# First two experts' rows by one-hot products, in two halves inside pair 0 of a mixture-of-experts trunk

## What is computed

```python
h = modulate(rmsnorm(x, norm2), sh2, sc2)              # h = xn2 * a + b, per channel
g_top, g_idx = lax.top_k(softmax(t @ w_router_g + b_router_g), 1)
e_top, e_idx = lax.top_k(e_logits_of_group, 2)
e_w = jax.nn.softmax(e_top) * g_top
# per expert e, over the tokens sent to it:
a = t @ w1[e];  b = t @ w3[e]                          # 1024 -> 256
out += ((silu(a) * b) * combine[:, e]) @ w2[e]         # 256 -> 1024
x = x + gate2 * out
```

## Time and profile before

| | us |
|---|---|
| median of 3 runs (648.75 to 650.32) | 650.08 |
| profiled execution | 645.07 |
| its span, first to last instruction | 643.0 |
| PE busy | 578.9 (90%) |
| DVE busy | 298.2 |
| ACT busy | 154.7 |
| POOL busy | 96.1 |

### The profile page before, as it was taken

One profiled execution on the slowest core, in us unless ns is written; L12 is line 12 of the kernel. 1 busy time (PEld: TensorE's weight loads), 2 busy tenths in 40 slices (PEclk: granted clock), 3 DMA queues, 4 the chain that ended last, 5 costly groups with the idle time before them and its releaser, 6 DMA issues.

```text
span 643.0 us, 7238 instructions
## 1 busy us (share of the span) xinstructions
PE 578.9 (90%) x2754; PEld 334.5 (52%) x2754; DVE 298.2 (46%) x580; ACT 154.7 (24%) x336; POOL 96.1 (15%) x144
## 2 busy tenths in 40 slices
PE   3899799999999999999999998999996888697991
PEld 1544486877766667764688843333332323232341
DVE  0229986446656564229524385323222222245258
ACT  3034022244334434332202302112111111111110
POOL 3032241079300000000000011111111111101000
PEclk9999899999999999999999989999998889899996
DMA  8995944311672506060556594999999999999873
GB/s 309 399 353 224 331 162 163 131 53 78 232 293 77 185 1 262 1 242 20 208 231 281 201 417 154 375 421 420 419 420 420 420 420 418 421 421 419 374 301 133
DMA packets 42647, 173.80 MB, mean 270 GB/s; under 512 B 6396, under 2 KB 6460, under 8 KB 30836
## 3 DMA queue, kind: packets, MB, share of 16 engines
q1 hardware_dynamic: 35280, 159.40, 62.7%
q0 software_dynamic: 5744, 12.84, 5.4%
q10 hardware_dynamic: 1588, 1.10, 0.5%
HBM read 165.36 MB, written 15.74 MB: 282 GB/s over the span
## 4 chain that ended last, share of the span: by engine, by line
PE 54%; SPq 18%; DMA 12%; issue 6%; DVE 6%; POOL 3%; ACT 0%; ACTq 0%; DVEq 0%; POOLq 0%
PE bank L945 8%; SPq L520 7%; SPq L532 6%; PE bank L656 5%; PE bank L658 5%; PE bank L657 5%; DMA late<-in_w_dram 4%; PE bank L746 4%; PE bank L982 4%; SPq L521 4%; DMA arena<-in_w_in_dram 3%; POOL ss L1927 3%; DMA late<-in_w_in_dram 3%; PE bank L840 2%; PE bank L841 2%
## 5 line engine op out<-in xcount | busy, mean ns | idle before, releaser
L945 PE MATMUL bank<-arena,hT 128*64 128x512 f32 x352 | 86.9, 637 | 13.3 <-issue 13.3
L656 PE MATMUL bank<-hT_high,w_in_parts 128*128 128x512 f32 x160 | 66.3, 414 | 0.0
L1667 DVE SCALAR_TENSOR_TENSOR g1b<-g1b,bank 128x256 f32<-128x256 f32 x16 | 6.7, 420 | 123.1 <-ACT g1b L1231 123.0
L658 PE MATMUL bank<-hT_high,w_in_parts 128*128 128x512 f32 x160 | 62.7, 392 | 0.0
L657 PE MATMUL bank<-hT_low,w_in_parts 128*128 128x512 f32 x160 | 62.4, 390 | 0.0
L945 PEld LDWEIGHTS bank<-arena,hT 128*64 128x64 f32 x352 | 26.3, 145 | 61.8 <-issue 60.4
L945 PE MATMUL bank<-late,hT 128*64 128x512 f32 x160 | 39.8, 643 | 10.7 <-issue 6.9
L982 PE MATMUL bank<-arena,g1b 128*64 128x512 f32 x176 | 40.2, 598 | 1.2 <-DVE acc L1691 1.2
L1958 POOL DMA_INDIRECT hT<-xn_scratch,gidx x16 | 16.4, 1028 | 137.6 <-PE bank L923 120.5
L1237 ACT COPY g1b<-bank 128x256 f32<-128x256 f32 x16 | 6.0, 372 | 128.5 <-PE bank L964 128.5
L1407 DVE TENSOR_REDUCE st<-bank 128x2 f32<-128x256 f32 (+3 forms) x16 | 13.2, 824 | 45.1 <-PE bank L682 45.1
(11 more groups left out here) (285 smaller groups left out, 946.3 us busy)
## 6 DMA issues: line engine op xcount, KB each, us to landing
arena<-in_w_dram SPq DMA_DIRECT2D x58, 1024.0 KB, 27.5
late<-in_w_dram SPq DMA_DIRECT2D x30, 1024.0 KB
late<-in_w_ada_dram SPq DMA_DIRECT2D x6, 2048.0 KB, 12.9
arena<-in_w_ada_dram SPq DMA_DIRECT2D x5, 2048.0 KB, 9.1
arena<-in_w_in_dram SPq DMA_DIRECT2D x4, 2048.0 KB, 11.0
late<-in_w_in_dram SPq DMA_DIRECT2D x4, 2048.0 KB, 17.9
arena<-in_w_dram SPq DMA_DIRECT2D x16, 512.0 KB, 9.3
y_scratch<-arena POOLq DMA_DIRECT2D x1, 4096.0 KB, 18.2
```

The costliest lines, as they stand in the source:

```text
L656: mm(bank[:, b, :], wH[:, b, k, :], hH[:, k, :], start=k == 0, stop=False)
L658: last = mm(bank[:, b, :], wL[:, b, k, :], hH[:, k, :], start=False, stop=k == 7)
L945: last = mm(bank[SLOTS * x:SLOTS * (x + 1), 2 + q % 2, :].rearrange("p (w f) -> p w f", w=2), xgT[q % 2][:, k, SLOTS * x:SLOTS * (x + 1)], ...
```

## The change

The rows of pair 0 no longer come by a gather. DVE makes a table `place0` in fp32 for the two experts of pair 0, and PE multiplies the tokens in SBUF by it (`first_rows`): for each k four products of 128x128 with 128 columns, summed over the four token tiles, which leaves the rows already transposed. Steps k 0 to 3 are made before `gate_up(0)`, with the sums of group 0 between; steps 4 to 7 stand inside `gate_up(0)`, after its k 3. They go to banks 0, 1, 3 and 6, the sums of groups 0 and 1 to the free parts of banks 4 and 5. `gather_transposes(1)` moves from after k 3 to after k 5 of `gate_up(0)`, `slot_sums(1)` to after k 6. Of the warming products around them (2, 3, 4 and 2) one is left. The sums of group 2 move from after k 0, 1, 2 of `gate_up(1)` to after k 3, 4, 5, the hidden transposes of pair 0 there from k 3 to k 5.

DVE makes one table of group 2 after pair 0's scaling, then the combine weights, and only when `first_rows` is done the tables of group 1, one more of group 2, indices 1, and pair 1's scaling; the third and fourth table of group 2 follow, the last one after `ab_done` of pair 0. POOL gathers from pair 1 on. The tiles of rows and tables move to other places in `g1b`, `hT`, `probs` and `acc`; those lines, and renamed offsets, are cut here.

```diff
+        first_bank = lambda k: bank[:, (0, 1, 3, 6)[k // 2], P * (k % 2):P * (k % 2 + 1)]
-            keep_warm(2, 5)
-            slot_sums(0)
-            keep_warm(3, 5)
-            slot_sums(1)
-            keep_warm(4, 5)
+            def first_rows(ks):
+                for k in ks:
+                    for t in range(TT):
+                        last = mm(first_bank(k), xn2[:, t, k:D:KT],
+                                  place0[:, t].rearrange("p e s -> p (e s)"), start=t == 0, stop=t == TT - 1)
+                    if k % 2 == 1:
+                        last.then_inc(xt_ready if k == KT - 1 else x0_done, 1)
...
                 for k in range(KT):
+                    if q == 0 and k == KT // 2:
+                        first_rows(range(KT // 2, KT))
+                        pe.wait_ge(xgT_act, 1)
                     if q == 0 and k < KT // 2:
                         pe.wait_ge(xgT_ready, k + 1)
-                    if q == 0 and k == KT // 2:
-                        pe.wait_ge(xgT_act, 1)
...
-                    if q == 0 and k == KT // 2 - 1:
+                    if q == 0 and k == KT - 3:
                         gather_transposes(1)
-                    if q == 1 and k < 3:
-                        slot_sums(2, IDX_GROUPS[2][4 * k:4 * k + 4])
-                    if q >= 1 and k == 3:
+                    if q == 0 and k == KT - 2:
+                        slot_sums(1)
+                    if q == 1 and 3 <= k < 6:
+                        slot_sums(2, IDX_GROUPS[2][4 * k - 12:4 * k - 8])
+                    if q >= 1 and k == (5 if q == 1 else 3):
                         hidden_transposes(q - 1)
...
-            pe.wait_ge(idx_ready, 1)
-            gather_transposes(0)
-            keep_warm(2, 5)
+            keep_warm(1, 5)
+            pe.wait_ge(place0_ready, 1)
+            first_rows(range(2))
+            slot_sums(0)
+            first_rows(range(2, KT // 2))
             all_pairs(step, near_end=lambda: counts.append(overflow_count(pe)))
...
-            dve.wait_ge(xn2_stored, 16 * TT)
+            v.tensor_tensor(place0, rm[:, :, 0:2].unsqueeze(3).broadcast_to([P, TT, 2, SLOTS]),
+                            iota_s.unsqueeze(1).unsqueeze(1).broadcast_to([P, TT, 2, SLOTS]),
+                            ALU.is_equal).then_inc(place0_ready, 1)
...
             indices(0)
-            one_hot(1, range(TT))
-            indices(1)
-            one_hot(2, range(0, 2))
...
             modulate_gathered(0)
+            one_hot(2, range(1))
...
             weights_of_last()
+            dve.wait_ge(xt_ready, 1)
+            dve.wait_ge(xn2_stored, 16 * TT)
+            one_hot(1, range(TT))
+            one_hot(2, range(1, 2))
+            indices(1)
             modulate_gathered(1)
-            one_hot(2, range(2, TT))
+            one_hot(2, range(2, 3))
+            dve.wait_ge(ab_done, 1)
+            one_hot(2, range(3, TT))
...
             pool.wait_ge(xn2_stored, 16 * TT)
-            for q in range(STORED + 5):
+            for q in range(1, STORED + 5):
...
-                        if q == qs[0]:
+                        if q == max(qs[0], 1):
                             pool.wait_ge(idx_ready, g_ + 1)
                     if q >= 2:
                         pool.wait_ge(xt_ready, q - 1)
```

More of the change, by code:

```diff
@@ L370, in hybrid_trunk @@
         xt_ready = sem("xt_ready")
+        place0_ready = sem("place0_ready")
+        x0_done = sem("x0_done")
         xgT_ready = sem("xgT_ready")
@@ L901, in slot_sums @@
                             lhs = place[g][t][:, e:e + 2, :].rearrange("p e s -> p (e s)")
-                            last = mm(idx_bank(g)[:, 64 + 6 * i:64 + 6 * i + 6], lhs,
+                            last = mm(idx_bank(g)[:, LASTW + 6 * i:LASTW + 6 * i + 6], lhs,
                                       cparts[:, t, 2 * i:2 * i + 2, :].rearrange("p e c -> p (e c)"),
@@ L1217, in modulate_gathered @@
             def modulate_gathered(q):
-                act.wait_ge(xt_ready, q + 1)
+                if q >= 1:
+                    act.wait_ge(xt_ready, q + 1)
                 if q >= 2:
@@ L1222, in modulate_gathered @@
                 for k in range(KT // 2, KT):
-                    last = sc.activation(xgT[q % 2][:, k, :], bank[:, 1, P * (k % 4):P * (k % 4 + 1)], ACT.Identity,
+                    if q == 0 and k == KT - 4:
+                        act.wait_ge(x0_done, 3)
+                    if q == 0 and k == KT - 2:
+                        act.wait_ge(xt_ready, 1)
+                    src = bank[:, 1, P * (k % 4):P * (k % 4 + 1)] if q else first_bank(k)
+                    last = sc.activation(xgT_of(q)[:, k, :], src, ACT.Identity,
                                          bias=ab2[:, 1, k:k + 1], scale=ab2[:, 0, k:k + 1])
@@ L1637, in weights_by_slot @@
                         r = slice(SLOTS * x, SLOTS * (x + 1))
-                        a = 64 + 6 * i + 3 * x
-                        last = v.tensor_reduce(cws[r, i:i + 1], bank[r, 7, a:a + 3], AX.X, ALU.add)
+                        a = LASTW + 6 * i + 3 * x
+                        last = v.tensor_reduce(cws[r, i:i + 1], idx_bank(2)[r, a:a + 3], AX.X, ALU.add)
                 last.then_inc(sidx_ready, 1)
@@ L1657, in modulate_gathered @@
                 for k in range(KT // 2):
-                    last = v.tensor_scalar(xgT[q % 2][:, k, :], bank[:, k // 4, P * (k % 4):P * (k % 4 + 1)],
+                    if q == 0 and k % 2 == 0:
+                        dve.wait_ge(x0_done, k // 2 + 1)
+                    src = bank[:, k // 4, P * (k % 4):P * (k % 4 + 1)] if q else first_bank(k)
+                    last = v.tensor_scalar(xgT_of(q)[:, k, :], src,
                                            ab2[:, 0, k:k + 1], ab2[:, 1, k:k + 1], ALU.mult, ALU.add)
@@ L1980, in _ @@
                         pool.wait_ge(xt_ready, q - 1)
-                    gather(xg[:, q % 2, :], gidx[:, q:q + 1], xg_loaded[q % 2])
+                    gather(xg_of(q), gidx[:, q:q + 1], xg_loaded[q % 2])
                 if q == PAIRS - 1:
@@ L1989, in overflow @@
                 pool.sem_inc(x_turns, 1)
-                gather(xg[:, 0, :], gidxx[:, :], x_rows)
+                gather(xg[0], gidxx[:, :], x_rows)
                 pool.wait_ge(x_y_drained, b + 1)
```

30 lines of the change are left out of this document (17 added, 13 removed).

## The result

| | before | after |
|---|---|---|
| median, same chip, 20 runs each | 648.51 (646.58 to 650.32) | 651.67 (649.45 to 657.28) |
| profiled execution | 645.07 | 650.40 |
| its span | 643.0 | 648.6 |
| PE busy | 578.9 | 584.7 |

The ratio is 1.0058 [1.0038, 1.0079]: the change makes the kernel 2.5 to 5.1 us slower, where 2.9 us faster was forecast. In the tables the numbers in brackets or after a median are the lowest and highest run or, behind a ratio, its 95% interval.

A forecast was written before the change was run, and what follows sets the result against it. A saturated weight stream, started by slots PE frees, was taken to bound the kernel. 4.1 us for 1.57 MB less, minus 1.2 us later start, gave 2.9 us off 650.08: 647.2 us, range 645.0 to 650.2.

The forecast's parts named there:

- What bounds the kernel: End of the kernel: a saturated weight stream, 420 GB/s from 420 us on, starting when PE frees the first ring slots.
- The table and the start of the rows: VectorE's new table before pair 0: takes 0.7 us, ready at 377.6, seen by PE at 377.7, when the rows start.
- The 64 instructions of the row products: PE's products for pair 0's rows: 0.116 us each, 7.4 us in all; bounds 0.113 and 0.136, the upper making 8.7 us.
- the second batch: Half loads freed at the end of pair 0's gate and up: at 395.0 us instead of 398.4.
- My rival: Row products' stride-8 weight loads not hidden: twice 0.116 us each, +4.5 us, 654.6 us; chance 0.07.
- The first batch: Half loads freed by the first four steps of pair 0's gate and up: 385.3 us instead of 393.8, 8.5 earlier.
- the old hole: Before the weight stream, 387 to 394 us: DMA share 0.11; 2.1 MB of half loads would run alone there, done by 392.
- The waits: PE stands still 1.1 us for ScalarE's scaling and 1.45 us for pair 1's; other tables and pair 2's gather in time.
- The sum in bytes: Weight stream: 1.57 MB less to move, 4.1 us, less a 1.2 us later start: 2.9 us earlier, 2.5 to 3.7.
- a delay after about 410 us costs nothing: PE delays after about 410 us cost nothing as long as the weight stream has work queued.
- The clock: PE clock falls at new waits; in pair 0's second half the gain shrinks to 1.2 us, 648.9 us; chance 0.12.
- The range: Whole kernel: 645.0 to 650.2 us, from the forecast's bounds with 0.8 us of run spread, clock and most zero cases included.

The follow-up runs named there:

- the kernel without halves: Kernel after with tokens laid out by k and all eight steps of row products ahead of `gate_up(0)`: 644.25 us, 0.9937 of before.
- the kernel with contiguous rows: Kernel after with row products reading 128 neighbouring channels as weights, so pair 0's result is wrong: 645.03 us, 0.9951 of before.
- pair 3: Kernel before with four more warming products inside pair 3's gate and up product: 647.85 us, 1.0008 of before.
- tokens by k: Normalised tokens written in the order of the k steps, here in the kernel before: 648.76 us, 1.0013; in the kernel after: 644.61 us, 0.9942 of before.
- delay between: Kernel before with four more warming products between k 3 and k 4 of `gate_up(0)`: 651.58 us, 1.0054 of before.
- delay ahead: Kernel before with four more warming products ahead of `gate_up(0)`: 652.11 us, 1.0044 of before.
- kept-warm kernel: Kernel before with two more warming products in PE's wait for pair 0's gathered rows: 646.62 us, 0.9977 of before.
- the kernels with the scaling moved: Kernel after, tokens laid out by k, pair 1's scaling ahead of indices 1: 645.41 us, 0.995 of before; also with rows in one piece: 644.04 us, 0.9931.
- The loads alone: Kernel of weight loads only, without the layer, 8 MB per stage: halves 188 and 240 GB/s at a burst's start, then 412; whole loads 426.
- that kernel: Kernel of PE product streams only, without the layer, at several strides and column counts: 0.112 us per instruction at stride 1, 0.238 at stride 8.

## Why the prediction was wrong, step by step

**What bounds the kernel: right.** The stream of weights, started by the slots that PE frees; 420 GB/s from 420 us on in both; the end 4.94 us later with the last landing.

**The table and the start of the rows: right.** 377.61 against 377.7.

**The 64 instructions of the row products: the term that was mis-sized.** Predicted 0.116 us each, bounds 0.113 and 0.136; measured 0.244. It is 64 x 0.128 = 8.2 us, and the whole miss of the second batch, 403.34 for 395.0, is 8.3. I took the price from a stream with the same shape but contiguous weights and the upper bound from transposes that do read at a stride of 8. Both rows are right, and neither is this operation: here transposes keep their pace at a stride of 8 (0.109 alone), and products of 128 columns pay twofold (0.238 against 0.112). My rival had place, price and mechanism in full: the 64 instructions, the stride of 8, "twice 0.116", +4.5 us. Measured, by the ratio, +3.8 us. I gave it 0.07 because of the transposes.

**The first batch: 8.5 us earlier was forecast, 4.4 came**, by the same term (32 of its 64 instructions, 4.1 us). The sum already gave nothing for its being that early (its bytes fit in the old hole either way), and the kernel without halves shows that.

**The waits: right.** 0.90 us for ACT's scaling (forecast 1.1), 1.48 for pair 1's (1.45); no wait for the tables of group 2, none for pair 1's gather. They were right because each was worked out as a difference between two engines' times, which the mis-sized term moved together.

**The sum in bytes: it holds with the right price put in.** The second batch at 403.34, and 0.8 us to start moving, is 9.5 us behind the 394.6 of before; less the 4.1 us for the bytes already moved that makes 5.4 us later, and the mark in the table reads 5.4. With the second batch 3.1 us earlier, as in the kernel with contiguous rows, where the forecast had 3.4, it gives 2.6; the mark reads 2.5, and the runs 3.2 (1.8 to 4.6). The claim that a delay after about 410 us costs nothing is borne out by pair 3 (+0.08%).

**The clock: the rival that did not come, in after.** Waits of 0.22, 0.90 and 1.48 us left it at 1.00 in each stretch from 386 to 470. It fell in the kernel *before*, though: in three of its variants (tokens by k, delay between, delay ahead) the transposes behind the wait of 2.06 to 2.60 us took 1.78 to 1.94 us instead of 1.14, at a granted clock of 0.5, the 1.2 GHz level; in its own profiled execution (2.17) and in pair 3's (2.10) not. The profiled execution of before, 645.07 us, is 3.4 us under its median of 648.51, and the after's, 650.40, 1.3 under its own. That before's ordinary execution includes the drop now and then, and the profiled one does not, would explain why the profiles differ by 5.3 us and the medians by 3.2. It is consistent with the kept-warm kernel's -0.23%, but not shown: that interval includes no change, and of the other executions only the clock's mean over the launch is on record, which does not say where it fell (0.971 in the profiled execution of before, 0.960 to 0.972 in the others). And it is not the only such place. The clock was lower near 28 us in five of the twelve profiled executions (0.79 on average from 25 to 33 us) and in pair 15 in six, in neither place in before and after. The kept-warm kernel's profiled execution, 649.36 us, had both of these and not the drop behind the gather, and lies 2.7 us above its median.

**The range.** Its base, 650.08 us, was the median of three runs; over twenty it is 648.51, so 2.9 us less would have been 645.6. And its lower limit does not follow quite from what it names: 3.7 us and 0.8 of spread under 650.08 make 645.6, not 645.2. Neither decides anything: 651.67 lies above all of it, and above the base.

**What stays open:** why the kernels with the scaling moved keep less in their profiled executions than their second batch gives, and how much of the low rate of 303 and 321 GB/s between 404 and 420 us is the slow start of the half loads. The loads alone show such a start, but gathers run beside them in the layer.

## What to carry to other kernels

A price taken from another row must match in every operand's access pattern and in the kind of instruction, not only in shape and type. Where a pattern differs, the upper bound has to leave room (here it was double), and the rival that says so deserves the weight of an unmeasured term. When a saturated stream sets the end, ask which release it waits for last while its queue is empty: here that was the second batch, and splitting the work to free the first one sooner only put more ahead of the second. A layout that makes weights contiguous (0.4 to 0.5 us more per tile on DVE) is cheap here beside 64 product instructions that load weights for every 128 columns and lose 0.126 us each to the stride.

## What the runs showed of the hardware

- fp32 products of 128 columns: 0.112 us an instruction with weights at stride 1, 0.119 at 2, 0.233 at 4, 0.238 at 8; with 36 columns 0.119 and 0.237 at strides 1 and 8; with 512 columns 0.429 at either; a moving operand at stride 8 0.233. Transposes 0.109 at strides 1 and 8. bf16 0.056 and 0.062 at strides 1 and 8.
- The 0.237 of the strided products with 36 columns was kept at a granted clock of 0.50, beside 0.238 for 128 columns at 1.00: the pace that the strided loads set was the same at both levels.
- The clock fell at 61.0 us of that kernel without a wait of PE, at the end of a stream of products with 36 columns.
- Behind a wait of PE of 2.1 to 2.6 us ahead of pair 0's gate and up the granted clock fell in three of the five profiled executions that have one there; behind waits of 0.4 to 1.5 us there it fell in none. In pair 15 it was lower at waits of 2.2 to 4.3 us in six of six, and at waits of 0.7 to 1.9 us in none of six.
- Half loads (4 KB pieces) move 188 to 244 GB/s in the first 4 us of a burst and 412 or more after 6 to 8 us; whole loads reach 401 in the third microsecond and then move 426.
